# The norm in front of the pooling mixer, half 0: sums of squares in one step instead of three

## What is computed

```python
def _rms_norm(x, g):
    xf = x.astype(jnp.float32)
    y = xf * lax.rsqrt(jnp.mean(xf * xf, axis=-1, keepdims=True) + EPS)
    return (y * g.astype(jnp.float32)).astype(x.dtype)
...
        h_lat = _modulate(_rms_norm(x, norm_pre_mix[i]), sh_m, sc_m)
...
        else:
            y_lat = _pool_mixer(h_lat, pool_w[j], pool_b[j], pool_scale[j], rows)
```

## Time and profile before

| | us |
|---|---|
| median of three runs | 2110.63 |
| lowest and highest | 2105.22, 2112.9 |
| the profiled execution, its own time | 2113.2 |
| its span, from the first instruction to the last | 2111.5 |

### The profile page before, as it was taken

How to read it: one execution, slowest core, us unless ns; L and a number is a source line. 1 busy time by engine, 2 the same in 40 slices (tenths; PEclk the granted TensorE clock), 3 DMA queues, 4 the chain that set the end, 5 groups by cost and what they waited for, 6 DMA issues and landing times. The chain is left out here.

```text
span 2111.5 us, 26627 instructions
## 1 busy us (share of the span) xinstructions
PE 2022.4 (96%) x9048; PEld 1660.1 (79%) x9048; DVE 1520.7 (72%) x1510; ACT 843.5 (40%) x1119; POOL 1297.1 (61%) x836
## 2 busy tenths in 40 slices
PE   7899999999899999999999999799999999999996
PEld 6677776877788888888888768678888888888885
DVE  7588888879677777777777774697556665676557
ACT  4576768447222323232222355472322233223322
POOL 4534244656777777877787462368766676667653
PEclk9999999999999999999999989799999999999998
DMA  7132322531222222222222400211111111111114
GB/s 310 65 115 79 114 79 90 199 140 60 70 90 83 86 89 89 71 89 96 92 70 89 169 31 11 90 51 64 46 50 60 60 40 50 60 60 47 51 41 160
DMA packets 55931, 179.68 MB, mean 85 GB/s; under 512 B 5040, under 2 KB 6352, under 8 KB 55248
## 3 DMA queue, kind: packets, MB, share of 16 engines
q1 hardware_dynamic: 55888, 179.13, 24.3%
HBM read 166.52 MB, written 12.58 MB: 85 GB/s over the span
## 5 line engine op out<-in xcount | busy, mean ns | idle before, releaser
L2090 DVE TENSOR_TENSOR Y<-Y,ps 128x1024 f32<-128x1024 f32 x336 | 406.3, 1219 | 36.8 <-PE ps L586 0.7
L1700 POOL TENSOR_TENSOR F_lo<-S,F_hi 128x1024 fp32r<-128x1024 f32 x44 | 106.9, 2430 | 336.8 <-ACT F_hi L1362 336.8
L586 PE MATMUL ps<-F_hi,WC_hi 128*128 128x512 f32 x736 | 230.3, 391 | 1.1 <-ACT Y L1400 1.1
L1337 ACT ACTIVATE S<-S 128x1024 f32<-128x1024 f32 x48 | 51.0, 1063 | 448.9 <-DVE S L2194 448.9
L1114 ACT ACTIVATE So_hi<-So_raw 128x512 fp32r<-128x512 f32 x132 | 82.5, 628 | 368.6 <-POOL So_raw L1575 365.9
L586 PE MATMUL ps<-F_hi,WC_lo 128*128 128x512 f32 x736 | 229.7, 390 | 0.0
L586 PE MATMUL ps<-F_lo,WC_hi 128*128 128x512 f32 x704 | 216.8, 389 | 0.0
L1678 POOL TENSOR_TENSOR So_lo<-So_raw,So_hi 128x512 fp32r<-128x512 f32 x132 | 189.3, 1461 | 5.5 <-ACT So_hi L1114 5.5
L586 PEld LDWEIGHTS ps<-F_hi,WC_hi 128*128 128x128 f32 x736 | 138.0, 188 | 30.3 <-ACT Y L1400 1.8
L586 PEld LDWEIGHTS ps<-F_hi,WC_lo 128*128 128x128 f32 x736 | 138.4, 188 | 28.8
L586 PEld LDWEIGHTS ps<-F_lo,WC_hi 128*128 128x128 f32 x704 | 132.2, 188 | 27.5
(11 more groups left out here) (302 smaller groups left out, 5382.1 us busy)
## 6 DMA issues: line engine op xcount, KB each, us to landing
rawA<-wA SPq DMA_DIRECT2D x62, 512.0 KB, 3.3
rawB<-wB SPq DMA_DIRECT2D x62, 512.0 KB, 3.3
E<-ada SPq DMA_DIRECT2D x46, 512.0 KB, 3.3
rawC<-wC SPq DMA_DIRECT2D x46, 512.0 KB, 3.8
quad<-ada SPq DMA_DIRECT2D x8, 2048.0 KB, 9.4
ada_first<-ada SPq DMA_DIRECT2D x4, 2048.0 KB, 15.5
outT<-X SPq DMA_DIRECT2D x16, 512.0 KB, 3.6
X<-outT SPq DMA_DIRECT2D x16, 512.0 KB, 7.1
```

The lines of the kernel that those rows point to most:

```text
L586: mm = pe.matmul(out, w[:, w_cols:w_cols + P], (hi, lo)[part], start=first and w is W_hi[s] and part == 0, stop=last and w is W_lo[s])
L1337: A(S[0][:], S[0][:], ACT.Gelu_apprx_tanh).then_inc(gelu_done, 1)
L1700: TT(dst[:], S[1][:], F_hi[:].bitcast(F32), ALU.subtract).then_inc(f_ready, 1)
L2090: TT(Y[:, m], Y[:, m], flat(ps[:, b:b + 2, :]), ALU.add).then_inc(d_added, 1)
```

## The change

`add_squares` no longer multiplies the squares by the identity: it calls `column_sums` on each of the eight as it is made, and all eight accumulate in the four result columns of bank 6. The ACT copy, its semaphore `acc_copied` and the column sums of the copy are gone. `acc_done` is now signalled by the last matmul of a square's column sums, for squares 0 to 6; the last square signals `ssq_done`, as the copy's sums did.

```diff
-            def column_sums(q, h, src, at, first, last):
+            def column_sums(q, h, src, at, first, last, added=None):
 
                 for t in range(4):
                     mm = pe.matmul(ps[:, ssq_bank(q, h), 4 * h + t:4 * h + t + 1], src[:, at + t * P:at + t * P + P],
                                    ones[:, 0:1], start=first and t == 0, stop=last and t == 3)
                 if last:
                     mm.then_inc(ssq_done[h], 1)
+                elif added is not None:
+                    mm.then_inc(added, 1)
...
-                else:
-                    pe.wait_ge(acc_copied, 1)
-                    column_sums(q, h, *total, True, True)
 
             def add_squares(q, h, ps_):
 
                 for p in ps_:
                     pe.wait_ge(sq_made[h], 8 * q + p + 1)
-                    pe.matmul(ps[:, 5], ident[:], square_cols(q, h, p), start=p == 0, stop=p == KT - 1)\
-                        .then_inc(acc_done, 1)
+                    column_sums(q, h, *square_slot(q, h, p), p == 0, p == KT - 1, acc_done)
...
             add_squares(4, 0, range(2, KT))
-            norm(4, 0)
+            spread(4, 0)
...
             squares_x(4, 1, 0, range(2, KT))
-            act.wait_ge(acc_done, KT)
-            A(square_cols(4, 0, 0), ps[:, 5], ACT.Copy).then_inc(acc_copied, 1)
             norm_root(4, 0)
```

More of the change, by code:

```diff
@@ L243, in build_trunk @@
         sum_both, sum_last = ([sem(f"{n}{h}") for h in range(2)] for n in ("sum_both", "sum_last"))
-        acc_done, acc_copied = sem("acc_done"), sem("acc_copied")
+        acc_done = sem("acc_done")
         ssq_done, rms_made = ([sem(f"{n}{h}") for h in range(2)] for n in ("ssq_done", "rms_made"))
```

## The result

The changed kernel takes 2113.44 us, the median of 20 runs (2106.73 to 2117.49), against 2109.18 us for the kernel before (20 runs, 2101.75 to 2113.76): a ratio of 1.0022, 95% interval 1.0012 to 1.0031, that is 2.5 to 6.5 us more. The forecast was 2114.4 us, slower by 0.2%, and counted as the same. The profiled execution of it took 2114.8 us from first to last instruction.

What follows compares the result with a forecast made beforehand. TensorE, busy 96% of the span, bounds the kernel; ahead of the mixer a serial chain does. Root +3.1, spread +0.9, earlier clock return -0.2 sum to +3.8 us on the median 2110.63: 2114.4 us, range 2107.0 to 2119.0.

Steps and rivals of the forecast that it cites:

- The level: TensorE's clock ahead of the pooling mixer: 1.2 GHz from about 1226.0 us to beyond the mixer's first products.
- The price of a square: Column sums of one square on TensorE: eight one-column products at 0.218 us, 1.74 us at the low clock.
- The root: Root of half 0's norm, after the last square's sums: at 1239.45 in place of 1236.32 us, +3.1 us.
- The spread: Second spread of 1/rms, half 0, ahead of the mixer: 2.08 us at the low clock for 1.16, +0.9 us.
- DVE and the mixer: DVE's mixer input at 1242.1 for 1238.04 us, +4.0; the mixer's first product at 1244.4 for 1240.35.
- What gives way: Under the mixer's first products: clock back after 5.75 us, before 6.1, giving back 0.2 us; may move by 1 us.
- The total: Whole program: +3.8 us, 2114.4 us against the median of three, slower by 0.2%, counted as the same; chance 0.76.
- A: Clock holds or returns during the squares' sums: root at 1232.8, -3.5 us, 2107.1 us; chance 0.09.
- B: Delay covered or halved, by a later low stretch or sooner clock return under the mixer: 0 to +2 us; chance 0.12.
- C: Clock doesn't come back under the mixer's first products: +21 us on top of +4, 2135.6 us; chance 0.03.

Runs made afterwards that it cites:

- the run with 128 columns: Changed kernel with 128 moving columns of ones in place of 1 in the eight squares' column sums; 0.998 of the kernel before.
- the run with fillers: Changed kernel plus one 512-column identity product, into an unread bank, ahead of the sums of each of squares 1 to 7; 1.009 of the kernel before.
- the run with both norms at 128 columns: Changed kernel with 128 moving columns in the eight squares' sums and in the FFN norm's half-1 sums; 0.9987 of the kernel before.
- the run with half the sums: Changed kernel with squares 4 to 7 of half 0 not summed; 0.9994 of the kernel before.
- the second profile: Changed kernel, unaltered, run again twelve times and profiled; ratio 1.0025 to runs of the kernel before made beside it.

## Why the prediction was right

**The level.** The step on which all hung, 1.2 GHz from about 1226 to the mixer, held in both profiles, and the run with 128 columns shows that it is the width of the products that makes it. That the fall came within 0.1 us of where I had it was luck: from the start it came at 4.9 us in both first profiles, but at 2.2, 2.5, 4.4 and 5.5 in the other four with narrow sums in the FFN's norm, and I had allowed 1.5 us either way. My argument for the return in the kernel before was coarser than the chip: I put it down to wide products filling TensorE. In the run with fillers wide products filled it by half, and the clock didn't come back; which property of the mixture decides is not shown. In the kernel before, wide ones and the 128-column spread followed each other between 1226 and 1229.5 with no narrow ones between them.

**The price of a square.** 1.74 us at the low level, taken from the earlier trace rows; in the profile after, six squares take 10.24 us less the tail of the last, 1.7 us each. And as forecast TensorE waits for no square behind the second: its 48 products run without a gap.

**The root.** Predicted at 1239.45, measured at 1239.50: 3.0 us later, counted from the sums, for 3.1. **The spread**: 2.08 us, as said. **DVE and the mixer**: +4.0 us each (17.0 to 21.0; 19.3 to 23.3), as said.

**What gives way.** I gave back 0.2 us for an earlier return of the clock under the mixer; in the first profile it came back 5.5 us after the mixer's first product for the 5.75 of the sum, and the half-1 sums are 3.7 us later than before. In the second, with the return at 3.2 us, the stretch from the mixer to the half-1 sums is 1.4 us shorter than before, outside the 1 us that I had allowed this term. Its middle was right for the first profile, its spread too small.

**The total.** +3.8 us forecast, +4.3 us measured between the medians, 4.6 by the ratio. The forecast's 2114.4 us is 1.0 us from the 2113.44 because two misses oppose each other: the median of three that it starts from lies 1.5 us above that of twenty, and the change cost 0.5 us more. Between the spans of the first two profiles it is +3.3 us, but executions of one kernel differ by up to 12 us, and the second profiled execution of the changed kernel was 3.9 us below that of the kernel before, so this agreement is luck. In the first pair the rest of the program is shifted by what this place costs, within 0.6 us.

**The rivals.** A, with the clock held, didn't occur in the changed kernel: the clock was low under the sums in both its profiles, with TensorE busy throughout. The runs that held it by width show that its arithmetic was also wrong: I had the root at 1232.8 and everything behind it 3.5 us earlier, and in fact DVE's queue takes back two thirds (the reciprocal starts 2.1 us after the root's end in the run with both norms at 128 columns, 1.9 in the run with half the sums). The step I missed is the reciprocal's place behind the updates of half 1, which in the kernel before are done 1.0 us ahead of it; without a change of DVE's order the reciprocal starts in no run before 14.4 us from the start. B's sooner return of the clock is real: in the second profile it came 2.5 us before the 5.75 of the sum, for the 3 us of B, and the half-1 sums were 2.0 us late, B's upper end. So B holds for single executions; the medians, +4.3 and a ratio of 1.0025 in the second set of runs, lie outside it. C didn't occur in any profile: wherever the clock was low under the mixer's first products, it came back 3.2 to 6.1 us behind the first of them, in the run with fillers too, after 35 us at the low level before the mixer.

## What to carry to other kernels

At the high clock a product by one column of ones takes as long as one by 128 columns, 0.114 and 0.112 us, so nothing in a profile warns of it. But in all six profiles with narrow sums in the FFN's norm the clock fell behind or under them, though not behind every such run, and at the low level each takes 0.213 us. Where sums over partitions come in long runs, it is worth trying 128 columns of ones as the moving operand: the same number of products and loads, and in the five kernels here that had them the clock came back under the sums or didn't fall there. And before shortening one link of a chain through several engines, look what stands ahead of the next link in its own queue.

## What was not expected of the hardware

Wide and narrow products in turn, 1.84 and 1.57 us of each without a gap, left the granted clock at 0.50 for 41 us; that a mixture which is half wide work doesn't bring the clock back I had not expected. It is one profile, and why the wide products and the spread of the kernel before did bring it back (at 8.3 us) is open. And the return under the mixer's products, the same instructions each time, took 5.5 us in one profile of the changed kernel and 3.2 in the other; with a fall that came 0.6 us later, that is 1.7 us of the time with no difference in the program.
